# Splitting the tokens 256/288 and streaming the high and low inputs of 256 tokens in one 512-column matmul

## The chip, the cores and the metric

One core of one Trainium2 chip. The metric is device time in microseconds of one launch. Times of the kernel before: 2362.09, 2362.61 and 2363.95 us, median 2362.61 us.

## The reference, cut to what matters

Two layers of a streaming encoder act on 512 prompt tokens and 32 sample tokens, with a model width of 1024:

```python
for l in range(DEPTH):                       # DEPTH = 2
    mods = silu(c) @ ada_w[l] + ada_b[l]     # 9*1024 columns: shift, scale, gate of three sub-layers
    h = modulated_pre(x, ..., 0); x = gated_post(x, swiglu(h, w1, w3, w2), ..., 0, 0.5)
    h = modulated_pre(x, ..., 1)
    z = h @ w_in[l]                          # queries, latent, retention q, k, v, gate
    # latent attention and retention on z, then
    x = gated_post(x, concat(o_mla, o_ret) @ w_out[l], ..., 1, 1.0)
    h = modulated_pre(x, ..., 2); x = gated_post(x, swiglu(h, w1, w3, w2), ..., 2, 0.5)
# modulated_pre: rms_norm(x)*g*(1+scale)+shift;  swiglu: (silu(h@w1) * (h@w3)) @ w2, D_FF = 2816
```

Everything is float32. The kernel gets near float32 precision from matmuls of type fp32r by splitting each factor in a high part (rounded to fp32r) and a low part (the rest), and adds three products: high weight with high input, high weight with low input, low weight with high input.

## The kernel before, in words

Activations lie feature-major: 128 features on the partitions, T = 544 tokens along the free axis. A weight tile is 128x128 and turns one block of 128 input features into 128 output features. For each such tile and input block the kernel runs one **k-step** (`tile3`, L662): the 544 tokens are cut in two halves of HT = 272, one per PSUM bank, and each half gets three matmuls, six in all. Where the result needs a shift term, the second half carries 4 more columns (HB = 276), in which the product of weights and shift appears. An output tile is an accumulation over 8 k-steps (up projections, z, output projection) or 22 (down projection), into two neighbouring banks.

Stages of a layer: up projections of the first FFN (`up`, L765, two output tiles w1 and w3 for each of 22 features), its down projection (`out_tiles`, L787, 8 tiles, the last by `last_tile`, L813, one half after the other), a turn-over (norm, gate, new h; `first_tiles`, L714, starts the next stage while h is being made), the mixer's 21 z tiles (`z_tile`, L855), attention and retention, the mixer's output projection, and the second FFN in the same way.

Around PE each engine has its own program in a fixed order:

- **SP** loads weight chunks in `raw`, two slots, and in the down stages the tiles of `ada_w` (a ring of four) between them.
- **ACT** makes `w_hi` of each chunk (`high` L1172, `high_at` L1178, both wait for the chunk of that slot to be used up), and after that, in the same program, evacuates: `tile` in `up` (L1294: silu, cast to `u_hi`), `z_out` (L1350), `tile` in `out_tiles` (L1317: square, scaled copies to `o_buf`). An evacuation that waits holds the next `high`.
- **POOL** makes `w_lo` of each chunk after that (`low`, L543) and adds squares.
- **DVE** multiplies the PSUM results with the inverse root-mean-square `rinv` (`ffn` L1640; `z_scaled` L1689) and copies the four bias columns next to them, does the gating, the rotary embedding (`turn`, L1725, whose operations stand between the calls of `z_scaled`), in the down stages the modulation products (`ada_group`, L1551), and the residual updates (`turn_over`, L1580).
- **PE** waits for `lo_done` of a chunk before its tile, for bank evacuation (`up_out`, `z_mul`, `out_ev`), and in the last tile's second half, at k = 2, for `ada_done` of all modulation products of the stage (`half_sums`, L690). `z_tile(3)` waits for the evacuation of z tile 1 (L870).

In the mixer ACT's order is: `high` of chunk z + 2, then `z_out` of tile z, which waits for DVE's `z_mul`. So the weights of tile z + 3 come only after DVE has multiplied tile z. In the early tiles a `square` follows each `z_out` (L1368).

```python
for t in range(2):                                    # tile3, L667
    n = slice(t * HT, t * HT + width[t])
    pe.matmul(ps[:, bank + t, 0:width[t]], wh, hi[:, n], start=start, stop=False)
    pe.matmul(ps[:, bank + t, 0:width[t]], wh, lo[:, n], start=False, stop=False)
```

## Time and profile before

| | |
|---|---|
| timed runs | 2362.09, 2362.61, 2363.95 us (median 2362.61) |
| profiled execution | span 2360.0 us from its first to its last instruction; its own time outside the span is not listed, the median lies 2.6 us above the span |
| PE | busy 2304.0 us, 98% of the span |
| PE weight loads | 2184.5 us, 93% |
| DVE | 1220.4 us, 52% |
| POOL | 880.6 us, 37% |
| ACT | 821.1 us, 35% |
| DMA queue q1 | 262.44 MB, 33.1% of 16 engines |
| mean granted TensorE clock | 0.981 |

Busy matmuls overlap, since each is shown from its start until its result has passed the array, so 98% says that PE rarely waits, not that it streams all the time. How fast PE goes is read from the distance between the starts of its matmuls. Shares of DVE and ACT are averages over stages: in some stretches they are fully busy.

### The profile page before, as it was taken

How to read it: one execution, taken by the hardware profiler on the slowest of the kernel's cores; microseconds unless marked ns; L12 is line 12 of the kernel's file. 1: busy time of each engine (PE TensorE's matmuls, PEld its weight loads, DVE VectorE, ACT ScalarE, POOL GpSimd, SP SyncE). 2: the span in 40 equal slices, each digit the busy share in tenths (PEclk: the TensorE clock that was granted, in tenths of full speed). 3: DMA queues.
4: the chain of work that ended last, by engine and by line, in shares of the span. 5: the costliest groups of instructions: out<-in, count | busy, mean ns of one | idle time of the engine just before them, and what ended most of it. 6: DMA issues, size and time to landing. Idle time of an engine off the chain costs nothing.

```text
span 2360.0 us, 43873 instructions
## 1 busy us (share of the span) xinstructions
PE 2304.0 (98%) x17694; PEld 2184.5 (93%) x17694; DVE 1220.4 (52%) x2065; ACT 821.1 (35%) x1392; POOL 880.6 (37%) x382
## 2 busy tenths in 40 slices
PE   8999999999999999999999999999999999999998
PEld 7999999899558899999999999999984699999998
DVE  5333379877561533338153333996846624333502
ACT  4323332433454433332243333225343553332321
POOL 2344334343113344344434334443321143433352
PEclk7999999999999999999999999999999999999999
DMA  6222268322211122236312223882231022222422
GB/s 233 90 83 86 89 238 312 136 86 81 73 37 54 60 84 89 89 113 246 123 58 86 89 89 110 296 289 75 82 111 51 1 72 73 88 89 89 163 86 75
DMA packets 70948, 263.82 MB, mean 112 GB/s; under 512 B 8704, under 2 KB 10112, under 8 KB 70336
## 3 DMA queue, kind: packets, MB, share of 16 engines
q1 hardware_dynamic: 70848, 262.44, 33.1%
q8 instruction: 69, 1.13, 0.2%
q14 instruction: 31, 0.25, 0.0%
HBM read 258.96 MB, written 3.45 MB: 111 GB/s over the span
## 4 chain that ended last, share of the span: by engine, by line
PE 75%; issue 10%; DVE 5%; POOL 4%; ACT 3%; DMA 1%; SPq 1%; POOLq 0%; DVEq 0%; ACTq 0%
PE ps L673 21%; PE ps L669 20%; PE ps L670 20%; POOL w_lo L546 4%; DVE wide_v L1561 2%; PE ps L679 1%; PE ps L745 1%; PE ps L1090 1%; PE ps L832 1%; PE ps L834 1%; PE ps L833 1%; PE ps L975 1%; DMA x<-in_x 1%; PE ps L1113 1%; PE ps L1057 1%
## 5 line engine op out<-in xcount | busy, mean ns | idle before, releaser
L546 POOL TENSOR_TENSOR w_lo<-raw,w_hi 128x1024 fp32r<-128x1024 f32 (+1 forms) x304 | 785.9, 2585 | 1296.2 <-ACT w_hi L1183 947.4
L669 PE MATMUL ps<-h_hi,w_hi 128*128 128x272 f32 x3296 | 886.8, 289 | 3.7 <-POOL w_lo L546 3.7
L670 PE MATMUL ps<-h_lo,w_hi 128*128 128x272 f32 x3296 | 889.4, 287 | 0.0
L673 PE MATMUL ps<-h_hi,w_lo 128*128 128x272 f32 x3296 | 685.7, 289 | 0.0
L669 PEld LDWEIGHTS ps<-h_hi,w_hi 128*128 128x128 f32 x3296 | 619.1, 188 | 5.2 <-POOL w_lo L546 5.0
L670 PEld LDWEIGHTS ps<-h_lo,w_hi 128*128 128x128 f32 x3296 | 620.9, 188 | 0.2
L1183 ACT CAST w_hi<-raw 128x1024 fp32r<-128x1024 f32 (+1 forms) x236 | 269.3, 1141 | 830.6 <-PE ps L673 809.0
L673 PEld LDWEIGHTS ps<-h_hi,w_lo 128*128 128x128 f32 x3296 | 519.2, 188 | 0.0
L669 PE MATMUL ps<-u_hi,w_hi 128*128 128x272 f32 x1232 | 332.7, 288 | 1.0 <-POOL w_lo L546 1.0
L670 PE MATMUL ps<-u_lo,w_hi 128*128 128x272 f32 x1232 | 332.4, 289 | 0.0
L1561 DVE CUSTOM_DVE_ANT_0 wide_v<-ada_w,ps,ada_b 128x1024 bf16<-128x1024 f32 x256 | 309.0, 1285 | 22.7 <-DMA ada_w<-in_ada 18.2
L1652 DVE TENSOR_TENSOR wide_v<-ps,rinv 128x544 f32<-128x544 f32 x88 | 63.8, 725 | 437.3 <-PE ps L673 437.3
L673 PE MATMUL ps<-u_hi,w_lo 128*128 128x272 f32 x1232 | 255.2, 288 | 0.0
L1657 DVE SCALAR_TENSOR_TENSOR wide_v<-wide_v,wide_s 128x512 f32<-128x512 f32 (+1 forms) x176 | 193.7, 1139 | 105.2 <-ACT wide_s L1300 105.2
L669 PEld LDWEIGHTS ps<-u_hi,w_hi 128*128 128x128 f32 x1232 | 231.7, 188 | 1.9 <-POOL w_lo L546 1.9
L670 PEld LDWEIGHTS ps<-u_lo,w_hi 128*128 128x128 f32 x1232 | 232.1, 188 | 0.0
L673 PEld LDWEIGHTS ps<-u_hi,w_lo 128*128 128x128 f32 x1232 | 192.8, 188 | 0.0
L1303 ACT CAST u_hi<-wide_v 128x544 f32 (+1 forms) x88 | 57.1, 649 | 213.6 <-DVE wide_v L1657 213.6
L1587 DVE RECIPROCAL tok_inv<-tok_root 128x3 f32<-128x3 f32 x12 | 2.1, 176 | 247.4 <-ACT tok_root L1191 247.4
L1176 ACT CAST w_hi<-raw 128x1024 fp32r<-128x1024 f32 x68 | 71.2, 1047 | 125.5 <-PE ps L673 82.5
L1662 DVE TENSOR_TENSOR u_lo<-wide_v,u_hi 128x544 f32 x88 | 63.8, 726 | 80.1 <-ACT u_hi L1303 80.1
L1300 ACT ACTIVATE wide_s<-wide_s 128x512 f32<-128x512 f32 (+1 forms) x176 | 82.2, 514 | 4.6 <-DVE wide_s L1649 4.6
(284 smaller groups left out, 2642.3 us busy)
## 6 DMA issues: line engine op xcount, KB each, us to landing
raw<-in_w_up SPq DMA_DIRECT2D x176, 512.0 KB, 3.5
ada_w<-in_ada SPq DMA_DIRECT2D x128, 512.0 KB, 5.2
raw<-in_w_dn SPq DMA_DIRECT2D x64, 704.0 KB, 4.8
raw<-in_w_mix SPq DMA_DIRECT2D x64, 512.0 KB, 3.6
ada_first<-in_ada SPq DMA_DIRECT2D x10, 512.0 KB, 7.8
decay<-in_decay SPq DMA_DIRECT2D x2, 2048.0 KB, 8.7
ada_first<-in_ada_first SPq DMA_DIRECT2D x6, 512.0 KB, 11.4
x<-in_x SPq DMA_DIRECT2D x4, 544.0 KB, 17.2
```

What stands on the lines that cost most here:

```text
L546: pool.tensor_tensor(w_lo[:, slot, 0:width], raw[:, slot, 0:width], w_hi[:, slot, 0:width].bitcast(F32), ALU.subtract).then_inc(lo_done.se ...
L669: pe.matmul(ps[:, bank + t, 0:width[t]], wh, hi[:, n], start=start, stop=False)
L670: pe.matmul(ps[:, bank + t, 0:width[t]], wh, lo[:, n], start=False, stop=False)
L673: last = pe.matmul(ps[:, bank + t, 0:width[t]], wl, hi[:, n], start=False, stop=stop)
L1176: nc.scalar.copy(w_hi[:, slot, 0:width], raw[:, slot, 0:width]).then_inc(hi_done.sem, 1)
L1183: nc.scalar.copy(w_hi[:, k, 0:width], raw[:, k, 0:width]).then_inc(hi_done.sem, 1)
L1300: nc.scalar.activation(wide_s[:, f, at], wide_s[:, f, at], ACT.Silu, bias=wide_s[:, f, T + 2 * v:T + 2 * v + 1]).then_inc(up_silu.sem, 1)
L1303: nc.scalar.copy(u_hi[:, bass.ds(i * 2 + f, 1), :].rearrange("p a n -> p (a n)"), tmp_v[:, f, :]).then_inc(up_hi.sem, 1)
L1561: v_.tensor_tensor_reduce(junk[v], ada_w[:, t, :], c_psum(v), 1.0, ada_b[:, b0 + t:b0 + t + 1], ALU.mult, ALU.add, mods[:, v, n0 + t:n0 + ...
L1652: v_.tensor_tensor(halves(tmp_v[:, f, :]), pair(4 * f + 2), halves(rinv[:, :]), ALU.mult)
L1657: v_.scalar_tensor_tensor(out=wide_v[:, f, at], in0=wide_v[:, f, at], scalar=wide_v[:, f, T + 2 * v:T + 2 * v + 1], in1=wide_s[:, f, at], ...
L1662: v_.tensor_tensor(u_lo[:, at, :].rearrange("p a n -> p (a n)"), tmp_v[:, f, :], u_hi[:, at, :].rearrange("p a n -> p (a n)").bitcast(F32) ...
```

## The change

The halves become TA = 256 and TB = 288 tokens. High and low parts of each input now lie in one buffer (`h_both`, `u_both`, `qn_both`, `mla_both`, `ret_both`), so that one matmul can stream the high and then the low part of the first 256 tokens against the high weights: 512 columns, into the two halves of one bank. The low half of that bank collects high weight x high input (and low weight x high input), the upper half high weight x low input. The two bank halves have to be added before use. ACT copies the low half to SBUF (`apart_sb` lies in `squares`, `apart_out` in `root`), DVE adds it to the upper half in place, and after that the 544 tokens lie contiguous over two banks, so that evacuations that took two or three instructions take one. The same holds for `first_tiles`, which writes high products to the low half and low products to the upper. `uq` and the last output tile of each projection keep three matmuls per part (`half3`).

```diff
-HT = T // 2
+TA = 256
+TB = T - TA
...
-            [("h_hi", [P, KD, HP], F32R), ("h_lo", [P, KD, HP], F32R)],
+            [("h_both", [P, 2, KD, HP], F32R)],
...
+        def part(b, t, more=0):
+            return ps[:, b + 1, 0:TB + more] if t else ps[:, b, 512 - TA:512]
+        def tokens(b, width=T):
+            return ps[:, b:b + 2, :].rearrange("p b n -> p (b n)")[:, 512 - TA:512 - TA + width]
+        def apart(b):
+            return ps[:, b, 0:TA]
...
+            def half3(bank, t, wh, wl, both, start, stop, more=0):
+                out, n = part(bank, t, more), slice(OFF[t], OFF[t] + WID[t] + (more if t else 0))
+                pe.matmul(out, wh, both[:, 0, n], start=start, stop=False)
+                pe.matmul(out, wh, both[:, 1, n], start=False, stop=False)
+                return pe.matmul(out, wl, both[:, 0, n], start=False, stop=stop)
...
+            def tile3_apart(bank, slot, kk, both, start, stop, more=4):
+                wh = w_hi[:, slot, kk * P:(kk + 1) * P]
+                wl = w_lo[:, slot, kk * P:(kk + 1) * P]
+                pe.matmul(ps[:, bank, :].rearrange("p (v n) -> p v n", v=2), wh, both[:, :, 0:TA], start=start, stop=False)
+                pe.matmul(apart(bank), wl, both[:, 0, 0:TA], start=False, stop=stop)
+                return half3(bank, 1, wh, wl, both, start, stop, more)
...
                 def tile(i, f, last_width, ahead=True):          # ACT, up
-                    for k in range(2) if ahead else ():
-                        high_at(l, base, i * 2 + f + 1, k, last_width if f else KD * P)
+                    for k in range(2):
+                        if ahead:
+                            high_at(l, base, i * 2 + f + 1, k, last_width if f else KD * P)
+                        else:
+                            used(l, base + k)
+                        nc.scalar.copy(apart_sb[:, k, :], apart(4 * f + 2 * k)).then_inc(up_apart.sem, 1)
...
                     act.wait_ge(w_used.sem, w_used.at(l, chunk0 + (m + 1) * per_tile))     # ACT, out_tiles
+                    nc.scalar.copy(apart_out[:, mm, :], apart(2 * mm)).then_inc(out_apart.sem, 1)
                     act.wait_ge(sq_added.sem, sq_added.at(l, j * SQ + N_EARLY + m - 1))
-                    nc.scalar.activation(halves(tmp_s[:, mm, :]), pair(2 * mm), ACT.Square).then_inc(out_sq.sem, 1)
+                    act.wait_ge(out_added.sem, out_added.at(l, j * (KD - 1) + m + 1))
+                    nc.scalar.activation(tmp_s[:, mm, :], tokens(2 * mm), ACT.Square).then_inc(out_sq.sem, 1)
...
                 def z_out(z, buf, dst, func=ACT.Identity):       # ACT, mixer
+                    used(l, MIX_C0 + z)
+                    nc.scalar.copy(apart_sb[:, buf, :], apart(z_bank(z))).then_inc(z_apart.sem, 1)
                     act.wait_ge(z_mul.sem, z_mul.at(l, z + 1))
...
+            def add_out(l, j, m):                                # DVE
+                dve.wait_ge(out_apart.sem, out_apart.at(l, j * (KD - 1) + m + 1))
+                b = 2 * (m % 2)
+                v_.tensor_tensor(part(b, 0), part(b, 0), apart_out[:, m % 2, :], ALU.add).then_inc(out_added.sem, 1)
+            def add_apart(b, slot, added, l, count):
+                v_.tensor_tensor(part(b, 0), part(b, 0), apart_sb[:, slot, :], ALU.add).then_inc(added.sem, 1)
+                dve.wait_ge(added.sem, added.at(l, count))
...
-                        v_.tensor_tensor(halves(tmp_s[:, f, :]), pair(4 * f), halves(rinv[:, :]), ALU.mult)
-                        v_.tensor_copy(wide_s[:, f, T:TW], biases(4 * f)).then_inc(up_out.sem, 1)
+                        dve.wait_ge(up_apart.sem, up_apart.at(l, 2 * n + 1))
+                        add_apart(4 * f, 0, up_added, l, 2 * n + 1)
+                        v_.tensor_tensor(wide_s[:, f, :], tokens(4 * f, TW), rinv[:, :], ALU.mult).then_inc(up_out.sem, 1)
...
+                    for i in range(ADA_A // ADA_RING):           # DVE, first FFN's down stage
                         ada_group(l, i, 16 + i * ADA_RING, i * ADA_RING, first_ffn=True)
+                        if i == 1:
+                            dve.wait_ge(ada_done.sem, ada_done.at(l, 2 * KD))
+                            post_columns(l, 0)
+                        if i % 3 and i < 11:
+                            add_out(l, 0, 2 * (i // 3) + i % 3 - 1)
...
                 def z_scaled(z):
-                    dve.wait_ge(w_used.sem, w_used.at(l, MIX_C0 + z + 1))
+                    dve.wait_ge(z_apart.sem, z_apart.at(l, z + 1))
...
-                    v_.tensor_tensor(halves(z_tmp[:, z % 2, 0:T]), pair(bank), halves(rinv[:, :]), ALU.mult)
-                    v_.tensor_copy(z_tmp[:, z % 2, T:TW], biases(bank)).then_inc(z_mul.sem, 1)
+                    add_apart(bank, z % 2, z_added, l, z + 1)
+                    v_.tensor_tensor(z_tmp[:, z % 2, :], tokens(bank, TW), rinv[:, :], ALU.mult).then_inc(z_mul.sem, 1)
```

In the second FFN's down stage `add_out` of tiles 0, 1, 2, 3, 4, 5 and 6 stands behind modulation groups 0, 1, 2, 3, 4, 5 and 5 (in the last layer only groups 0 and 1 exist). In the mixer the seven `add_out` stand behind all other DVE work.

## Rows read from the trace of the kernel before

**Rows 1.** The page: busy time, and the chain that ended last.
```profile
PE 2304.0 (98%) x17694; PEld 2184.5 (93%) x17694; DVE 1220.4 (52%) x2065; ACT 821.1 (35%) x1392; POOL 880.6 (37%) x382
PE 75%; issue 10%; DVE 5%; POOL 4%; ACT 3%; DMA 1%; SPq 1%; POOLq 0%; DVEq 0%; ACTq 0%
```
**Rows 2.** Groups by line and shape: line, instruction, count, busy us, mean ns.
```profile
L669 PE MATMUL ps<-h_hi,w_hi 128*128 128x276 f32 x1648 | 477.7, 290 | 0.0
L669 PE MATMUL ps<-u_hi,w_hi 128*128 128x272 f32 x1232 | 332.7, 288 | 1.0 <-POOL w_lo L546 1.0
L669 PE MATMUL ps<-ret_hi,w_hi 128*128 128x272 f32 x112 | 30.4, 289 | 0.0
L669 PE MATMUL ps<-mla_hi,w_hi 128*128 128x272 f32 x112 | 30.2, 288 | 0.0
```
**Rows 3.** Timeline of ACT: start us, length us; weight casts that wait for PE.
```profile
401.70 1.38 ACT L1183 CAST w_hi<-raw 128x1408 fp32r<-128x1408 f32 x1 [5.48 <-PE ps L673]
...
426.56 1.38 ACT L1183 CAST w_hi<-raw 128x1408 fp32r<-128x1408 f32 x1 [6.91 <-PE ps L673]
...
813.76 1.05 ACT L1183 CAST w_hi<-raw 128x1024 fp32r<-128x1024 f32 x1 [4.99 <-PE ps L673]
...
825.84 1.05 ACT L1183 CAST w_hi<-raw 128x1024 fp32r<-128x1024 f32 x1 [4.90 <-PE ps L673]
```
**Rows 4.** Window at half clock (PEclk 0.50), PE's timeline in it, and float32 matmuls.
```profile
777.00:780.40 3.40, 1.95 (x8) 1.75 (x8) 2.65 (x8) 3.40 (x9) 2.37 (x1) 0.50 0.18 74
...
779.07 0.43 PE L728 MATMUL ps<-h_hi,w_hi 128*128 128x272 f32 x1
...
779.53 0.43 PE L728 MATMUL ps<-h_hi,w_hi 128*128 128x272 f32 x1
...
604.68 3.60 PE L920 MATMUL ps<-kv,k_tok 128*128 128x512 f32 x8
608.12 1.45 PE L930 MATMUL ps<-w_ukv,kv 128*128 128x512 f32 x3
```
**Rows 5.** Timeline of DVE and ACT in the z tiles of layer 0.
```profile
521.34 0.72 DVE L1695 TENSOR_TENSOR z_tmp<-ps,rinv 128x544 f32<-128x544 f32 x1 [0.50 <-PE ps L673]
...
572.93 0.72 DVE L1695 TENSOR_TENSOR z_tmp<-ps,rinv 128x544 f32<-128x544 f32 x1
...
574.60 1.04 ACT L1176 CAST w_hi<-raw 128x1024 fp32r<-128x1024 f32 x1
```
**Rows 6.** Windows: DVE's busy time in one stretch of the z tiles; PE after it.
```profile
545.00:557.00 12.00, 12.00 (x96) 11.79 (x94) 11.81 (x15) 3.88 (x6) 5.21 (x2) 1.00 0.28 83
...
578.15 0.39 PE L669 MATMUL ps<-h_hi,w_hi 128*128 128x272 f32 x1 [0.72 <-POOL w_lo L546]
```
**Rows 7.** Timeline of ACT and DVE at the first z tiles.
```profile
474.30 0.71 DVE L1695 TENSOR_TENSOR z_tmp<-ps,rinv 128x544 f32<-128x544 f32 x1
474.41 0.73 ACT L1352 ACTIVATE zq<-z_tmp 128x512 f32<-128x512 f32 x1 [3.23 <-DVE z_tmp L1696]
475.38 0.66 ACT L1357 ACTIVATE wide_s<-zq 128x544 f32<-128x544 f32 x1
476.25 0.72 DVE L1695 TENSOR_TENSOR z_tmp<-ps,rinv 128x544 f32<-128x544 f32 x1 [1.17 <-PE ps L673]
```
**Rows 8.** Timeline at the end of the first down stage: last DVE products, PE's half sums.
```profile
434.23 1.29 DVE L1561 CUSTOM_DVE_ANT_0 wide_v<-ada_w,ps,ada_b 128x1024 bf16<-128x1024 f32 x1
436.31 0.72 PE L686 MATMUL ps<-ones,squares 128*128 128x1 f32 x6
```
**Rows 9.** Timeline at the third down tile: ACT waits, PE's first matmul.
```profile
337.74 0.84 ACT L1330 ACTIVATE o_ffn<-ps,mul_post 128x272 f32<-128x272 f32 x2 [9.25 <-DVE mul_post L1575]
343.39 0.40 PE L669 MATMUL ps<-u_hi,w_hi 128*128 128x272 f32 x1 [0.27 <-POOL w_lo L546]
```
**Rows 10.** Groups by shape nearest to the added operations.
```profile
L1605 DVE TENSOR_TENSOR x<-x,ps 128x272 f32<-128x272 f32 x96 | 42.0, 438 | 3.3
L1330 ACT ACTIVATE o_ffn<-ps,mul_post 128x240 f32<-128x240 f32 x28 | 13.0, 463 | 0.0
```

More of the change, by code:

```diff
@@ L664, in tile3 @@
+            def tile3(bank, slot, kk, both, start, stop):
                 wh = w_hi[:, slot, kk * P:(kk + 1) * P]
                 wl = w_lo[:, slot, kk * P:(kk + 1) * P]
[L666 to L670 removed]
@@ L671, in tile3 @@
-                for t in range(2):
-                    n = slice(t * HT, t * HT + width[t])
-                    last = pe.matmul(ps[:, bank + t, 0:width[t]], wl, hi[:, n], start=False, stop=stop)
-                return last
+                half3(bank, 0, wh, wl, both, start, stop)
+                return half3(bank, 1, wh, wl, both, start, stop)
+            def tile3_apart(bank, slot, kk, both, start, stop, more=4):
[4 more added lines that the diff above has]
+                return half3(bank, 1, wh, wl, both, start, stop, more)
@@ L860, in z_tile @@
                     for k in range(KD):
[L861 removed]
+                        last = tile3_apart(bank, slot, k, h_both[:, :, k, :], k == 0, k == KD - 1)
                     last.then_inc(w_used.sem, 1)
@@ L1940, in _ @@
                 mixer(l)
+                for m in range(KD - 1):
+                    add_out(l, 1, m)
                 turn_over((l, 1, o_mix), (l, 2))
```

195 lines of the change are left out of this document (95 added, 100 removed).

## The prediction, made before the changed kernel was run

> **What bounds the kernel now.** The page's busy shares come first: PE 98%, DVE 52%, and 75% of the chain that ended last is PE [rows 1]. So the pace of PE's matmuls is the first term, and the question behind it is where another engine is already just in time. The groups by shape give the number of k-steps. L669 runs twice in each: 1648 x 2 calls with h make 1648 k-steps, u 616, the mixer's output projection 56 + 56, in all **2376** that become `tile3_apart` [rows 2]. Of the 1648, the loops give 1344 to the up projections (42 tiles x 8, four times) and 304 to the z tiles (19 x 8, twice).
>
> The pace: in the up stage two weight casts that wait for PE lie 12.08 us apart, 16 k-steps, so 755 ns each. In the down stage 24.86 us hold 33 k-steps, 753 ns each [rows 3]. At 2.4 GHz the columns alone would take 1644 / 2.4 = 685 ns and 1632 / 2.4 = 680 ns. So each of the six matmuls takes about 12 ns more than its columns. At the lower clock (0.50) two matmuls of 272 take 0.46 us, 230 ns each against 227 for the columns [rows 4]: there the excess is gone. The float32 matmuls, which stream at half rate, take 3.44 / 8 = 430 ns for 512 columns, against 427: also nearly nothing [rows 4]. The excess thus shows only where the stream (113 ns) is short and fast.
>
> **Term 1: five matmuls in place of six.** The columns stay the same (512 + 256 + 3 x 292 = 1644). What the sixth matmul and its weight load are worth isn't in the trace, so it is bounded:
>
> - nothing, if the excess goes with columns streamed at this rate and not with instructions;
> - 12 ns, if it is the same for each matmul;
> - 37 ns, if short matmuls are held to about 125.5 ns each whatever their width, while one of 512 streams at 213 + 3: 755 - (216 + 4 x 125.5) = 37.
>
> Between them the widths speak: the up step has 12 columns more than the down step, 5 ns of streaming, and takes only 2 ns more. That lies between a floor (0) and a fixed excess (5), so I take the middle between 12 and 37, **25 ns**. TensorE: Matmul & The Clock Gate in the Trainium skill (Back-to-back issue gap) gives N/2.4 + 2.5 ns per matmul; by it six would now take 700 ns where the rows show 755, and the saving would be 2.5 ns. The measured pace decides here, but the rule is a rival below.
>
> **Term 2: where a faster PE is not asked for.** Four places.
>
> *z tiles.* From 521.34 us on DVE never waits again until z tiles 16 and 17 at 572.93 [rows 5]; it is full of rotary operations, 11.81 of 12 us [rows 6]. The multiply of tile 16 frees ACT, which casts chunk 19 at 574.60, and PE resumes at 578.15 after a wait [rows 5, 6]. So the end of the z stage is DVE's, and each addition before it counts. One z tile now has an add of 256 columns in PSUM (0.44 us by L1605, [rows 10]; start to start about 0.4 once the wait for its own result is in) and loses the bias copy (0.07), so +0.4 us with the pipelining wait: 8 tiles from 9 to 16, 3.2 us. The start of the stretch moves too. DVE no longer starts on PE's signal but behind ACT's cast (1.05) and a copy (0.46, [rows 10]): +1.5. And at z tile 1 ACT copies the low half only after scaling and squaring tile 0: before, tile 1's multiply began at 474.30, in front of ACT's tile-0 work [rows 7]; now it is z_mul(0) at 474.8, scaling 0.95, square 0.66, copy 0.4, add and multiply 1.2: about 478.1. PE's z tile 3 waits for that and would have started when tile 2 was done, 476.2 [rows 7]: +2.0 us. Tiles 7 to 9, the latents' root in between, take the 2.0 and the 1.5 minus PE's gain by then (8 tiles x 8 x 25 ns = 1.6) and minus the 0.5 that DVE waited: about 2.1 in all with the adds at 7 and 8. So the z stage ends 3.2 + 2.1 = **5.3 us later** in each layer, and only the last two tiles' 16 k-steps of 152 gain.
>
> *First FFN's down stage.* The 48 modulation products keep DVE busy until 435.5, 0.8 us before PE's half sums, which wait for all of them [rows 8]. Seven `add_out` of 0.45 make 3.15 us, and the stage's first product starts 0.5 later, as ACT's copy precedes the last silu: DVE ends 125.7 + 3.65 = 129.4 us behind the stage's start (309.8) where PE was at 126.5. PE waits there however fast it was: **+3.0 us** in each layer, and its 308 k-steps gain nothing.
>
> *Second FFN's down stage.* ACT evacuates tile 0 only when `mul_post` is there (a 9.25 us wait until 337.74); cast, then POOL's low part, then PE's tile 2 after a wait at 343.39 [rows 9]. One or two adds (0.45 each) stand before it: tile 2 starts **0.85 us later**, the 44 k-steps before it gain nothing, 110 do. Twice.
>
> *Clock.* PE now stands still 3 to 5 us at the half sums. In the turn-over around 777 us the granted clock was at 0.50 after waits of that kind, for 3.4 to 6.8 us [rows 4]; 227 instead of 125.5 ns per matmul over 3.4 us loses 1.5 us, over 6.8 us 3.1. I take 2.5, twice.
>
> **Costed at nothing.** The adds and copies in the up stage: one feature's chain is cast 1.05, copy 0.46, add 0.44, multiply 0.7, gating 2.2, cast 0.65, in all 5.5 us before ACT is free, where a tile takes 5.8 us; and the next chunk has 2 us of slack behind that. If that cover goes, ACT's lateness reaches POOL's `w_lo` and PE. The output projection: copy, add, square, two copies are 3 us against a bank needed 6 us later. Merged instructions save DVE and ACT time off the path. The split 256/288 moves 0.4 us from one half of the last tile to the other; bounds -3 and +3 us over all six turn-overs. SP's queue issues the same DMAs in the same order; the `ada_w` loads behind later products can hold a `w_dn` load, with some 6 us in hand.
>
> **The sum.** K-steps that count: 1344 + 2 x 16 + 2 x 110 + 112 = 1708. Gain 1708 x 25 ns = 42.7. Costs 2 x 5.3 + 2 x 3.0 + 2 x 0.85 + 2 x 2.5 = 23.3. Net -19.4 us against the span of 2360.0, 2340.6; the median lies 2.6 above the span: **2343 us**.
>
> **Rivals.**
>
> - *Floor for short matmuls* (37 ns): 63.2 us gained. z costs 4.5 (more gain by tile 9), clock 3: 9 + 6 + 1.7 + 6 = 22.7. Net -40.5: 2322. For it: the flat step from 680 to 685 ns of columns, no excess at half clock. Against: a float32 weight load paces nothing at 427 ns, so no row shows the floor itself. Chance 0.20.
> - *Fixed 12 ns per matmul*: 20.8 gained; z costs 6.2, clock 2: 12.4 + 6 + 1.7 + 4 = 24.1. Net +3: 2366, no difference that counts. For it: it is the plain reading of 755 - 685. Against: the same excess is missing at half clock and in float32. Chance 0.22.
> - *Slower: DVE's chains without the gain.* The mechanism is DVE's queue in the z stage, its 48 products in the down stage: the price is 14.4 + 6 + 1.7 + 3 = 25 us if a k-step saves nothing (the excess goes with columns, as a stream slowed by the weight load beside it would show). It decides when a k-step saves less than 25 / 1708 = 14 ns. Then 2388. For it: DVE's full windows [rows 5, 6] and 0.8 us of slack [rows 8] are facts, the 25 ns a guess. Against: 12 columns more cost 2 ns, not 5. Chance 0.15. The Trainium skill's rule above, which leaves 2.5 ns for the sixth matmul, would gain 4 and land at 2383, beside this rival; its pace is contradicted by the 755 ns.
> - *The change doesn't do what it says*: the 512-column matmul, whose moving operand is two pieces far apart, costs more than its columns. At 25 ns more per step it ends like the last. Chance 0.05; no row has such an operand on the fp32r path.
>
> **How the numbers follow.** Forecast 0.38, with its own range 2333 to 2355. A measurement of this kernel can tell about 0.2%, 4.7 us, from no change. Faster: the forecast, the floor and a tenth of the fixed case, 0.60. Same: 0.14. Slower: 0.26, the last two rivals and a third of the fixed case. The range from 2316 to 2378 holds forecast, floor and fixed case with the unknown waits, and leaves out most of the two slower cases.
>
> **What would show it.** Casts that wait for PE in the up stage 16 x 730 = 11.7 us apart (11.5: floor; 11.9: fixed; 12.1: nothing). Starts of a 512-column matmul and the next 216 ns apart, or 225. PE's wait before z tile 19 longer, its first z tiles with a new gap of 2 us behind tile 2. In the first down stage a new wait of PE at L695 of 3 to 5 us and clock 0.50 behind it. Wrong would be: no wait there, DVE waiting for PE in the z tiles beyond tile 9, or new waits for `w_lo` in the up loops.

## The result, and the profile after

The changed kernel takes **2387.86 us** (median of 4 runs, 2387.33 to 2388.86) against 2363.28 for the kernel before beside it: ratio 1.0102, 95% interval 1.009 to 1.0114. It is **slower by 1.0%**. The forecast was 2343 us, faster. The profiled execution has a span of 2387.1 us against 2360.0. So the two traces differ by 27 us, where the medians differ by 24.6; the profiled execution of the changed kernel was its slowest.

The page, where [rows 1] stand for before:

```profile
PE 2307.4 (97%) x15288; PEld 2078.8 (87%) x15288; DVE 1249.4 (52%) x2108; ACT 888.5 (37%) x1610; POOL 882.7 (37%) x382
PE 75%; issue 11%; DVE 6%; POOL 4%; ACT 3%; DMA 1%; SPq 1%; POOLq 0%; DVEq 0%; ACTq 0%
```

2406 matmuls and weight loads fewer, and PE is busy 3 us *longer*. The groups by shape of the changed kernel, for [rows 2]; columns as there:

```profile
L698 PE MATMUL ps<-h_both,w_hi 128*128 128x512 f32 x1648 | 653.9, 397 | 11.5 <-POOL w_lo L564 7.8
L684 PE MATMUL ps<-h_both,w_hi 128*128 128x292 f32 x1648 | 491.4, 298 | 0.0
L699 PE MATMUL ps<-h_both,w_lo 128*128 128x256 f32 x1648 | 460.0, 279 | 0.0
L1586 DVE TENSOR_TENSOR ps<-ps,squares 128x256 f32<-128x256 f32 x218 | 94.2, 432 | 600.3 <-ACT squares L1321 530.2
```

The change does what it says: 1648 matmuls of 512 columns on `h_both` (the others read `u_both`, `mla_both` and `ret_both`), 218 additions of 0.43 us in the up stages and z tiles. The mean lengths overlap (a matmul is counted until it has drained), so the pace is read from starts. PE's timeline in an up loop of the changed kernel (start us, length us):

```profile
299.67 0.39 PE L698 MATMUL ps<-h_both,w_hi 128*128 128x512 f32 x1
299.90 0.28 PE L699 MATMUL ps<-h_both,w_lo 128*128 128x256 f32 x1
300.02 0.30 PE L683 MATMUL ps<-h_both,w_hi 128*128 128x292 f32 x1
300.15 0.30 PE L684 MATMUL ps<-h_both,w_hi 128*128 128x292 f32 x1
300.29 0.30 PE L685 MATMUL ps<-h_both,w_lo 128*128 128x292 f32 x1
300.42 0.39 PE L698 MATMUL ps<-h_both,w_hi 128*128 128x512 f32 x1
```

From 299.67 to 300.42 is one k-step, 0.75 us. Over the loops from 100 to 300 us the mean gaps between starts are 234 ns for 512 columns, 117 for 256, 134.6 for 292. Two casts on ACT that wait for PE, 16 k-steps apart, say the same with more digits:

```profile
285.52 1.05 ACT L1204 CAST w_hi<-raw 128x1024 fp32r<-128x1024 f32 x1 [4.64 <-PE ps L685]
...
297.60 1.05 ACT L1204 CAST w_hi<-raw 128x1024 fp32r<-128x1024 f32 x1 [4.72 <-PE ps L685]
```

12.08 us, as in [rows 3]: 755 ns with five matmuls, 755 with six. **The sixth matmul and its weight load were worth nothing.**

Where the 27 us are, from the starts of PE's stages in the two traces (us):

| stage | before | after | more |
|---|---|---|---|
| up stages, four together | 1116.7 | 1117.8 | 1.1 |
| first FFN's down stage to the mixer's tile 0, layer 0 | 137.5 | 146.2 | 8.7 |
| the same, layer 1 | 137.4 | 145.5 | 8.1 |
| z tiles, layer 0 | 143.0 | 148.2 | 5.2 |
| z tiles, layer 1 | 142.7 | 147.6 | 4.9 |
| q and attention, both | 264.6 | 266.2 | 1.6 |
| output projections, both | 105.4 | 103.6 | -1.8 |
| second FFN's down stages and what follows them | 275.7 | 275.1 | -0.6 |

(The 1.6 us of the attention part are not the change's: that part takes 131.5 or 133.1 us in one layer or the other of several of the kernels below, without a pattern. The up stages' 1.1 lie in the later ones.)

Two stages make it, and PE's waits name them. The waits of the changed kernel (line waited at, cause, us in total, times, longest):

```profile
PE ps L698 <- POOL w_lo L564: 12.2, 10, 1.5
PE ps L711 <- DVE mods L1599: 10.5, 2, 5.2
PE ps L698 <- DVE z_tmp L1742: 3.6, 2, 1.8
```

The second and third didn't exist before. The second is PE's half sums at the end of each first down stage, waiting for DVE's modulation products. PE's timeline there, and windows around it (us, PE busy, PEld busy, DVE, ACT, POOL, granted clock, DMA share, GB/s), changed kernel:

```profile
441.50 0.98 PE L711 MATMUL ps<-ones,squares 128*128 128x1 f32 x4 [5.24 <-DVE mods L1599]
```
```profile
426.30:441.50 15.20, 9.05 (x75) 8.64 (x74) 15.16 (x29) 3.77 (x7) 4.59 (x2) 0.92 0.58 194
441.50:445.00 3.50, 3.50 (x15) 3.50 (x16) 0.60 (x7) 0.26 (x1) 0.00 (x0) 0.50 0.01 2
445.00:448.40 3.40, 3.40 (x16) 3.38 (x16) 1.44 (x4) 0.00 (x0) 0.00 (x0) 0.50 0.00 0
448.40:451.80 3.40, 3.40 (x24) 3.40 (x24) 3.26 (x10) 1.80 (x5) 0.67 (x1) 0.88 0.00 0
```

DVE is busy in 15.16 of 15.20 us while PE stands for 5.2; then PE runs at 0.50, the 1.2 GHz level, for 7.7 us: two whole windows, and the first 0.8 us of the third, whose mean is 0.88. In layer 1 the same wait of 5.2 us is followed by 6.2 us at 0.50. [Rows 8] had PE arrive 0.8 us *after* DVE. The third wait is z tile 3's for z tile 1's multiply; DVE and PE there:

```profile
484.80 0.43 DVE L1586 TENSOR_TENSOR ps<-ps,squares 128x256 f32<-128x256 f32 x1 [1.95 <-ACT squares L1376]
486.05 0.50 PE L698 MATMUL ps<-h_both,w_hi 128*128 128x512 f32 x1 [1.82 <-DVE z_tmp L1742]
```

DVE in turn waits 1.95 us for ACT's copy. In layer 0 the clock falls behind this wait too (the window behind the wait, and the one after it):

```profile
486.80:490.20 3.40, 3.40 (x14) 3.11 (x14) 1.16 (x2) 2.11 (x5) 1.53 (x1) 0.50 0.00 0
490.20:493.60 3.40, 3.40 (x25) 3.22 (x24) 0.00 (x0) 0.85 (x2) 0.86 (x1) 1.00 0.41 139
```

That is 14 matmuls in 3.4 us where the next window has 25, some 1.5 us lost. In layer 1 the wait is as long, 1.82 us, and no such window follows. The rest of the z stage's loss lies at its end: PE's waits for `w_lo` there add up to 3.9 us in each layer, against 1.9 and 1.8 before. For layer 0 this makes 1.8 + 1.5 + 2.0 = 5.3 us where 5.2 were measured; in layer 1 about 1 us of the 4.9 stays unassigned.

### The profile page after: what moved, and what is told of

Its sections match the earlier page's. It is cut to its first block, busy times and chain, and to the rows that moved or that the text cites. A ratio compares the mean times of both kernels' runs of the same rounds, so it can differ in the third digit from the quotient of the medians.

```text
span 2387.1 us, 39345 instructions
## 1 busy us (share of the span) xinstructions
PE 2307.4 (97%) x15288; PEld 2078.8 (87%) x15288; DVE 1249.4 (52%) x2108; ACT 888.5 (37%) x1610; POOL 882.7 (37%) x382
## 4 chain that ended last, share of the span: by engine, by line
PE 75%; issue 11%; DVE 6%; POOL 4%; ACT 3%; DMA 1%; SPq 1%; POOLq 0%; DVEq 0%; ACTq 0%
PE ps L698 19%; PE ps L684 12%; PE ps L683 12%; PE ps L685 12%; PE ps L699 9%; POOL w_lo L564 3%; DVE wide_v L1599 2%; PE ps L705 1%; PE ps L771 1%; PE ps L1111 1%; PE ps L996 1%; DVE ps L1640 1%; DMA x<-in_x 1%; PE ps L1009 1%; PE ps L1134 1%
## 5 line engine op out<-in xcount | busy, mean ns | idle before, releaser
L698 PE MATMUL ps<-h_both,w_hi 128*128 128x512 f32 x1648 | 653.9, 397 | 11.5 <-POOL w_lo L564 7.8
L684 PE MATMUL ps<-h_both,w_hi 128*128 128x292 f32 x1648 | 491.4, 298 | 0.0
L685 PE MATMUL ps<-h_both,w_lo 128*128 128x292 f32 x1648 | 489.8, 297 | 0.0
L683 PE MATMUL ps<-h_both,w_hi 128*128 128x292 f32 x1648 | 489.1, 297 | 0.0
L699 PE MATMUL ps<-h_both,w_lo 128*128 128x256 f32 x1648 | 460.0, 279 | 0.0
L683 PEld LDWEIGHTS ps<-h_both,w_hi 128*128 128x128 f32 x1648 | 309.2, 188 | 75.2
L698 PEld LDWEIGHTS ps<-h_both,w_hi 128*128 128x128 f32 x1648 | 309.8, 188 | 13.6 <-POOL w_lo L564 9.3
L699 PEld LDWEIGHTS ps<-h_both,w_lo 128*128 128x128 f32 x1648 | 310.5, 188 | 0.2
L685 PEld LDWEIGHTS ps<-h_both,w_lo 128*128 128x128 f32 x1648 | 310.2, 188 | 0.0
L684 PEld LDWEIGHTS ps<-h_both,w_hi 128*128 128x128 f32 x1648 | 310.1, 188 | 0.0
L698 PE MATMUL ps<-u_both,w_hi 128*128 128x512 f32 x616 | 244.3, 397 | 4.3 <-POOL w_lo L564 4.3
L683 PE MATMUL ps<-u_both,w_hi 128*128 128x288 f32 (+1 forms) x792 | 235.4, 297 | 3.6 <-POOL w_lo L564 3.6
L684 PE MATMUL ps<-u_both,w_hi 128*128 128x288 f32 (+1 forms) x792 | 235.6, 297 | 0.0
L685 PE MATMUL ps<-u_both,w_lo 128*128 128x288 f32 (+1 forms) x792 | 234.5, 296 | 0.0
L683 PEld LDWEIGHTS ps<-u_both,w_hi 128*128 128x128 f32 x792 | 150.7, 190 | 32.3 <-POOL w_lo L564 4.5
L684 PEld LDWEIGHTS ps<-u_both,w_hi 128*128 128x128 f32 x792 | 150.9, 191 | 0.0
```

Source lines behind the costliest of these rows:

```text
L683: pe.matmul(out, wh, both[:, 0, n], start=start, stop=False)
L684: pe.matmul(out, wh, both[:, 1, n], start=False, stop=False)
L685: return pe.matmul(out, wl, both[:, 0, n], start=False, stop=stop)
L698: pe.matmul(ps[:, bank, :].rearrange("p (v n) -> p v n", v=2), wh, both[:, :, 0:TA], start=start, stop=False)
L699: pe.matmul(apart(bank), wl, both[:, 0, 0:TA], start=False, stop=stop)
```

## Experiments

The theory after the result (A): a k-step's time goes with its columns, not its instructions, and the slowdown is the added copies and additions in two places, the z tiles and the first down stage. The rivals: a saving that is there and eaten by waits; a 512-column matmul slower for its operand in two pieces; other parts of the change (split, layout) that cost. Times are medians; each ratio is to the kernel before, run on the same chip, with its 95% interval.

| kernel | us | before beside it | ratio |
|---|---|---|---|
| changed kernel | 2387.86 | 2363.28 | 1.0102 (1.009 to 1.0114) |
| two256 | 2388.61 | 2362.43 | 1.0105 (1.0089 to 1.012) |
| undo_z | 2379.45 | 2362.43 | 1.0068 (1.0054 to 1.0082) |
| undo_down0 | 2367.89 | 2362.43 | 1.0023 (1.0014 to 1.0032) |
| split_only | 2360.40 | 2362.43 | 0.9988 (0.9979 to 0.9997) |
| undo_z_down0 | 2359.58 | 2361.18 | 0.9990 (0.9981 to 0.9999) |
| z1_early | 2381.00 | 2361.18 | 1.0080 (1.0067 to 1.0094) |
| copy_first | 2382.87 | 2361.18 | 1.0090 (1.0076 to 1.0104) |
| two_moves | 2377.11 | 2362.55 | 1.0064 (1.0052 to 1.0076) |
| two_columns | 2359.11 | 2362.55 | 0.9985 (0.9976 to 0.9994) |
| bias_high | 2358.38 | 2362.55 | 0.9981 (0.9972 to 0.999) |

### two256: the sixth matmul back, and nothing else

```diff
-pe.matmul(ps[:, bank, :].rearrange("p (v n) -> p v n", v=2), wh, both[:, :, 0:TA], start=start, stop=False)
+pe.matmul(apart(bank), wh, both[:, 0, 0:TA], start=start, stop=False)
+pe.matmul(part(bank, 0), wh, both[:, 1, 0:TA], start=False, stop=False)
```

> The changed kernel with the 512-column matmul of each k-step split back into two of 256 columns with the same weights (high inputs into the half apart, low inputs into the token half); six matmuls and a sixth weight load as before the change, everything else (banks, copies, additions, 256/288) as in the changed kernel. Theory A, a stream of this type costs 0.46 ns per column whatever its width and an instruction costs nothing: 2388 us within 3, k-steps of 16 in the up stage 12.08 us as before. My forecast's step, 25 ns for the sixth matmul: 1708 k-steps that count make it 2388 + 43 = about 2430. A fixed 12 ns per matmul: about 2408. A rival, that the 512-column matmul with its operand in two pieces was slower than two of 256 (by 10 ns or more per k-step): below 2371.

Ratio 1.0105 against 1.0102: no difference, and 2376 matmuls and loads more. Its casts on ACT:

```profile
285.79 1.05 ACT L1205 CAST w_hi<-raw 128x1024 fp32r<-128x1024 f32 x1 [4.64 <-PE ps L685]
...
297.87 1.05 ACT L1205 CAST w_hi<-raw 128x1024 fp32r<-128x1024 f32 x1 [4.72 <-PE ps L685]
```

12.08 us again. This decides the first term by itself: 25 ns per k-step would be 43 us, even 12 ns would be 20. Nor is the operand in two pieces slow, since it takes what two matmuls take.

### undo_z: the z tiles back to six matmuls, no copy, no addition

```diff
 # PE, z_tile
-last = tile3_apart(bank, slot, k, h_both[:, :, k, :], k == 0, k == KD - 1)
+last = tile3(bank, slot, k, h_both[:, :, k, :], k == 0, k == KD - 1, 4)
 # ACT, z_out
-used(l, MIX_C0 + z)
-nc.scalar.copy(apart_sb[:, buf, :], apart(z_bank(z))).then_inc(z_apart.sem, 1)
 # DVE, z_scaled
-add_apart(bank, z % 2, z_added, l, z + 1)
 ...  (first_tiles of the mixer writes to the token halves; DVE waits for PE's tile, not for the copy)
```

> The changed kernel with the z tiles alone taken back to six matmuls into one token half each, without the copy on ACT and the addition on DVE; up, down and output stages stay changed. Theory A (DVE's and ACT's added work ends the z stage later, the sixth matmul is worth nothing): z stages 144.5 us instead of 149.4, so 2388 - 10 = 2378. Rival B (the z stage is longer for another reason, such as the wider second half or the new order of ACT's evacuations): 2388 within 2. Rival C (a k-step did save 10 to 25 ns, eaten elsewhere): z tiles slower by 152 x 2 x 10 to 25 ns = 3 to 7.6 us, so 2381 to 2386.

Ratio 1.0068: 0.0034 or 8 us gone. By PE's stages the z tiles take 142.4 and 143.5 us instead of 148.2 and 147.6, 9.9 us together. That is before's time (143.0 and 142.7): rival B, another cause in the z stage, falls. So does rival C, a saving eaten elsewhere, which wanted z tiles 1.5 to 3.8 us slower per layer than before. PE's waits for `z_tmp` are gone, and those for `w_lo` at the stage's end are back to 1.9 us.

### undo_down0: the first down stage back

```diff
 # PE, out_tiles: j == 0 is the first FFN's
-last = tile3_apart(2 * mm, ...)
+last = (tile3 if j in (0,) else tile3_apart)(2 * mm, ...)
 # ACT: copy to apart_out, wait for out_added
+if j not in (0,):
 # DVE, add_out
+if j in (0,):
+    return
```

> The changed kernel with the first feed-forward's down stage alone (both layers) taken back: six matmuls into the token halves, no copy on ACT, no addition on DVE between the 48 modulation products. Theory A (the seven additions and the waits for ACT's copies push the products past PE's half sums, and the standstill then costs PE its clock): down stage and half sums back to 126.5 us and the turn-over to 9.4, 8 to 9 us per layer: 2388 - 17 = 2371, no wait of PE for the products at the half sums, granted clock above 0.9 behind them. Rival B (the loads of the modulation weights are what come late, pushed by the other layout): the wait stays, 2386 to 2389. Rival C (only the wait goes, the clock falls anyway): 2388 - 11 = 2377.

Ratio 1.0023: 0.0079 or 19 us gone, the largest part. Down stage and turn-over take 136.6 us in both layers (after 146.2 and 145.5). PE at its half sums, and the windows behind them:

```profile
436.01 0.50 PE L715 MATMUL ps<-ones,squares 128*128 128x1 f32 x4
```
```profile
426.30:436.00 9.70, 8.83 (x74) 8.63 (x73) 9.05 (x22) 3.23 (x6) 4.52 (x2) 1.00 0.46 162
436.00:439.40 3.40, 3.40 (x30) 3.40 (x29) 0.62 (x3) 0.44 (x2) 0.00 (x0) 1.00 0.03 5
```

No wait, and the granted clock stays 1.00 where it was 0.50: 30 matmuls in 3.4 us, not 15. So the standstill costs twice, once as itself and once as the clock behind it, and with the wait both go. Rivals B (late loads) and C (the clock falls anyway) are out. (One stretch of 3.4 us at 0.50 later in the turn-over, from 456.8 us, is no part of it: the kernel before has it too, from 459.3 us.)

### undo_z_down0 and split_only: the two together, and all of it

undo_z_down0 is the two edits above together. split_only goes on: no 512-column matmul, copy or addition in the up stages, second down stages and output projections either.

> Both undone, the z tiles and the first feed-forward's down stage; up stages, second down stage and output projection keep the 512-column matmul, 1904 of the 2376 k-steps. Theory A (the two parts are all of the slowdown, and add up: -9 and -20 alone): 2388 - 29 = 2359, as split_only's 2360.4. Rival B (the up and second down stages cost or gain something too): a difference of over 4 us from split_only. My forecast's 25 ns would by now have shown as 1904 x 25 ns = 48 us, 2313.

> The split 256/288 and the operands with high and low in one tensor, but no 512-column matmul anywhere: six matmuls per k-step into the token halves, no copy and no addition in any stage; merged evacuations stay. Theory A (a k-step's time goes with its columns; all of the slowdown is the added copies and additions): 2388 - 10 - 17 - 1 and the output projection's 2 back = 2359 to 2363, no difference from the kernel before. Rival B (the new split or layout itself costs some us): 2366 to 2375. My forecast's term, 25 ns per k-step: about 2400.

0.9990 and 0.9988: both parts account for the whole slowdown, and add up (0.0034 + 0.0079 = 0.0113; together 0.0112). The 1904 k-steps that keep the five matmuls in undo_z_down0 neither gain nor lose against split_only. The split 256/288 with its merged evacuations is worth 0.1%, which the intervals just tell from nothing.

### z1_early: one copy moved on ACT

```diff
 # ACT, z_out
-used(l, MIX_C0 + z)
-nc.scalar.copy(apart_sb[:, buf, :], apart(z_bank(z))).then_inc(z_apart.sem, 1)
+for y in ((0, 1), (), (2,))[z] if z < 3 else (z,):
+    used(l, MIX_C0 + y)
+    nc.scalar.copy(apart_sb[:, y % 2, :], apart(z_bank(y))).then_inc(z_apart.sem, 1)
```

> The changed kernel with one instruction on ACT moved: the copy of z tile 1's half apart comes right behind that of tile 0, ahead of tile 0's scaling and square; nothing is removed. Theory A (2.1 us of PE's gap behind z tile 2 is this copy in ACT's queue, and DVE, which has little idle time from tile 7 to the end of the stage, carries it to the end): the gap behind z tile 2 falls from 2.1 to about 0.1 us and the stage ends 1.5 to 2.1 us sooner in each layer, 2388 - 4 = 2384. Rival B (DVE's root and latents in between swallow it, as the later part of the stage is bound by the additions alone): the gap goes but the stage's end stays, 2387 to 2388. Rival C (the gap has another cause): gap and time stay.

Ratio 1.0080, so about 5 us gone (0.0022). ACT's two copies now stand together, and DVE adds tile 1 right behind tile 0's multiply, 2.3 us sooner than at 484.80:

```profile
478.89 0.64 ACT L1377 COPY squares<-ps 128x256 f32<-128x256 f32 x2
...
481.85 0.73 DVE L1743 TENSOR_TENSOR z_tmp<-ps,rinv 128x548 f32<-128x548 f32 x1
482.49 0.42 DVE L1587 TENSOR_TENSOR ps<-ps,squares 128x256 f32<-128x256 f32 x1
```

PE's gap is gone, and the z tiles take 144.7 and 145.4 us, 3.5 and 2.2 less. That the first layer gave back more than the gap of 1.8 us is the clock: the changed kernel had 3.4 us at 0.50 behind the gap, about 1.5 us lost, and here the window at that place is at full clock:

```profile
486.80:490.20 3.40, 3.40 (x24) 3.19 (x23) 1.16 (x2) 1.09 (x3) 2.37 (x1) 1.00 0.03 6
```

So a single copy in the wrong place was over half of the z stage's loss (5.7 of 10.1 us). What is left goes with the additions and the other copies: PE's waits for `w_lo` at the stage's end are still 3.9 us here, and 1.9 in undo_z, which has neither additions nor copies. Which of the two holds them was not tested apart; that it is the additions on a full DVE is argued from [rows 5, 6].

### copy_first: the copy ahead of a cast in the down stages

```diff
 # ACT, out_tiles
-for k in range(2):
-    high_at(l, chunk0, m + 1, k, chunk_tiles * P)
+high_at(l, chunk0, m + 1, 0, chunk_tiles * P)
 act.wait_ge(w_used.sem, ...)
 nc.scalar.copy(apart_out[:, mm, :], apart(2 * mm)).then_inc(out_apart.sem, 1)
+high_at(l, chunk0, m + 1, 1, chunk_tiles * P)
```

> The changed kernel with ACT's copy of the half apart in the two feed-forward down stages moved ahead of the second of the two weight casts of each tile (before: behind both). Theory A (two of the seven additions find DVE waiting, 1.93 and 3.03 us, for a copy that stands behind a cast of 1.38 us; the rest of that wait is PE's tile end): DVE gains 1 to 1.4 us at each of the two, PE's wait of 5.5 us at the half sums becomes 2.7 to 3.5, and 2388 - 2 x 2.4 = about 2383. Rival B (DVE waits for the end of PE's tile, the copy's place hardly matters): 2387 to 2388. Rival C (a cast 0.36 us later makes POOL's low part and PE's next tile late): above 2390.

In the changed kernel two of the seven additions find DVE waiting for the copy, which stands behind a cast (timeline of DVE and ACT in the changed kernel, then that of DVE in copy_first, then PE's wait there: us in both layers together, times, longest):

```profile
378.75 0.43 DVE L1582 TENSOR_TENSOR ps<-ps,root 128x256 f32<-128x256 f32 x1 [1.93 <-ACT root L1349]
...
410.08 1.38 ACT L1204 CAST w_hi<-raw 128x1408 fp32r<-128x1408 f32 x1 [6.87 <-PE ps L685]
411.36 0.36 ACT L1349 COPY root<-ps 128x256 f32<-128x256 f32 x1
411.75 0.43 DVE L1582 TENSOR_TENSOR ps<-ps,root 128x256 f32<-128x256 f32 x1 [3.03 <-ACT root L1349]
```
```profile
378.09 0.43 DVE L1583 TENSOR_TENSOR ps<-ps,root 128x256 f32<-128x256 f32 x1 [0.66 <-ACT root L1348]
...
411.09 0.43 DVE L1583 TENSOR_TENSOR ps<-ps,root 128x256 f32<-128x256 f32 x1 [3.40 <-ACT root L1348]
```
```profile
PE ps L711 <- DVE mods L1600: 7.4, 2, 3.7
```

PE's wait fell from 5.2 to 3.7 us, by 1.5, not by the 2 to 2.8 expected. The first addition's wait shrank, but the second grew from 3.03 to 3.40: what it waits for is the end of PE's tile 5, which no cast delays. Half of the theory holds: the cast was worth 1.3 us once, and the rest is that `add_out` of tile 5 stands in DVE's list before PE has tile 5. Still the two stages with their turn-overs are 3.2 and 2.5 us shorter, more than the wait's 1.5, as the granted clock behind the shorter standstill came back sooner:

```profile
440.80:444.20 3.40, 3.36 (x18) 3.40 (x19) 0.64 (x7) 0.26 (x1) 0.00 (x0) 0.64 0.01 2
444.20:447.60 3.40, 3.40 (x25) 3.38 (x24) 2.13 (x6) 0.22 (x1) 0.00 (x0) 0.86 0.00 0
```

By the ratio, 1.0090, the gain is 0.0012, and the two intervals overlap. Both moves together:

> The changed kernel with both moves on ACT, that of z1_early (alone -6.5 against the changed kernel, beside runs of the kernel before) and that of copy_first (alone -4.5). Theory A (both are waits for ACT's order, in different stages): they add up, 2377. Rival B (one gives back the other, as the clock or the loads shift): 2380 or more. Either way slower than the kernel before, since the additions themselves stay.

1.0064, so 0.0038 or 9 us gone: they add up (0.0022 + 0.0012), and it stays slower than before, as theory A has it.

### pace, pace2, pace3: PE by itself

Three kernels with nothing but matmuls, with 128 x 128 weights where not said, each section behind a warm-up of 24 matmuls of 512 columns. Each ran once, pace3 on another chip than the other two. Their core (pace) is

```python
for i in range(48):
    last = pe.matmul(ps[:, i % 4, 0:n], wr[:, i % 4, :], xr[:, 0, i % KD, 0:n], start=True, stop=True)
```

> Matmuls alone; the whole computation is left out. Sections of 48 or 64 matmuls with 128 x 128 weights, each behind a warm-up of 24 of 512 columns, no other engine at work: fp32r with 512, 384, 272, 256, 128 and 64 columns, with two pieces of 256 far apart, with 32-column weights, and bf16 with 512 and 256. Theory A (column law, 0.46 ns per column at full clock and nothing per instruction): start to start 235 ns for 512, 177 for 384, 125 for 272, 118 for 256, 59 for 128 as long as the weight load does not take over; pieces as contiguous. Rival B (the excess over columns / 2.4 is contention with the other engines' work in the kernel): alone 512 columns take 213 to 216 ns and 256 take 107 to 110. Rival C (the weight load beside the stream slows it): 32-column weights give 0.42 ns per column where 128-column ones give 0.46. bf16: 0.42 ns per column if the slower pace belongs to fp32r, 0.46 if to every stream on this chip.

> Matmuls alone again; the whole computation is left out. Single widths 264, 276, 288, 292, 272 accumulating, and whole k-steps (16 each, banks and weights alternating as in the kernels) in the order of the kernel before (272 + 272, six matmuls), of the changed kernel (512 + 256 + 3 x 288, 290 or 292, five), with the 512 split into two of 256, and of split_only (3 x 256 + 3 x n, six). What is open: in the kernels 1644 columns take 755.0 ns per k-step in four different forms, 1632 take 750.0 or 753.3, and 1638 (two_columns) take 756.7, so 0.46 ns per column doesn't hold to a few columns. Theory A (the pace is PE's own): the same figures appear alone, 753 for old_272, 750 for new_288 and two_288, 755 for new_292 and split_292, 756.7 for new_290. Rival B (the other engines' traffic adds to it): all are shorter alone, by 10 to 15 ns (six times 123.3 = 740 for old_272; 230 + 117 + 3 x 131 = 740 for new_288), and five matmuls may be shorter than six by the 4 ns that one of 512 took less than two of 256.

> Matmuls alone a third time; the whole computation is left out. Alone, single widths in multiples of 16 took 117.0 (256), 123.3 (272) and 130.2 ns (288), 10 above columns / 2.4, but whole k-steps took 749.3 to 752.6 in every form, 8 to 12 ns above the sum of their widths. Which part of the mixture adds that: one bank for successive matmuls (one_bank, bank_5), the same weights again (one_weight, weight_5), the same input (one_input), another start of the input (input_272, input_264) or of the output (out_240), or different widths in a row (mixed_6, mixed_alt, mixed_5)? Theory A (it is the change of width or of start): mixed_6 at 749 per six and mixed_5 at 749 per five, one_bank and one_weight at 123.3. Rival B (successive matmuls into one bank): one_bank about 125.4, mixed_5 at 738, bank_5 at 749. Rival C (the weights): one_weight shorter or longer by 2 ns. If mixed_5 alone is 738 and mixed_6 742, the sixth matmul is worth 4 ns by itself and the k-step's form takes it back.

Mean start to start at full clock, ns, fp32r unless said:

| columns | ns | above columns / 2.4 |
|---|---|---|
| 256 | 117.0 | 10.3 |
| 264 | 121.6 | 11.6 |
| 272 | 123.3 | 10.0 |
| 276 | 126.6 | 11.6 |
| 288 | 130.2 | 10.2 |
| 292 | 135.0 | 13.3 |
| 384 | 174.9 | 14.9 |
| 512 | 230.0 | 16.7 |
| 512 in two pieces | 230.0 | 16.7 |
| 128 | 110.8 | 57.5 |
| 64 | 111.6 | 84.9 |
| 512, 32-column weights | 226.7 | 13.4 |
| 256, 32-column weights | 116.6 | 9.9 |
| bf16, 256 and 512 | 109.4, 215.8 | 2.7, 2.5 |

The pace is slower than the columns with no other engine at work, so rival B, contention, falls. The excess *grows* with the width: 10 at 256, 17 at 512. Hence one matmul of 512 saves not a fixed 10 ns against two of 256 but 4 (234.0 against 230.0). The same 256 columns took 118.3 in pace3, so such figures hold to about 1 ns. With 32-column weights the excess shrinks by 3.3 ns of 17 at 512 columns and 0.4 at 256, so rival C, the weight load, is not the main cause either. Below 256 columns there is a floor: 128 and 64 columns both take about 111 ns.

With bf16 the excess is 2.5 to 2.7 ns. That is the rule of the Trainium skill which the prediction set against the trace (TensorE: Matmul & The Clock Gate, Back-to-back issue gap), and it holds for bf16 here, not for fp32r. That section of the Trainium skill gives it as the gap of an isolated matmul, and about 131 ns at 512 columns for a stream of weight loads and matmuls. The bf16 part of pace is such a stream, and took 215.8.

In the 64-column section the granted clock fell to 0.50 while PE never stood still (windows of pace; it has no DVE, so the columns are us, PE, PEld, ACT, POOL, clock, DMA share, GB/s):

```profile
98.10:104.10 6.00, 6.00 (x56) 6.00 (x54) 0.00 (x0) 0.00 (x0) 1.00 0.00 0
104.10:107.50 3.40, 3.40 (x14) 3.15 (x14) 0.00 (x0) 0.00 (x0) 0.50 0.02 5
```

At that level, seen once, 64 columns took 213.5 ns and the 512 columns behind them 427: the floor doubles, and the excess over the columns is gone, as [rows 4] had shown for 272.

Whole k-steps in pace2, with banks, weights and order as in the kernels; its timeline for the form of the changed kernel with 288:

```profile
109.85 0.40 PE L203 MATMUL ps<-xr,wr 128*128 128x512 f32 x1
110.08 0.28 PE L205 MATMUL ps<-xr,wr 128*128 128x256 f32 x1
110.20 0.56 PE L171 MATMUL ps<-xr,wr 128*128 128x288 f32 x3
110.60 0.39 PE L203 MATMUL ps<-xr,wr 128*128 128x512 f32 x1
```

| form | matmuls | columns | ns alone | in a kernel |
|---|---|---|---|---|
| 272 x 6 (before, down) | 6 | 1632 | 752.6 | 753.3 |
| 512, 256, 3 x 288 (changed, down) | 5 | 1632 | 749.7 | 750.0 |
| the same, 512 as two of 256 (two256, down) | 6 | 1632 | 749.6 | 750.0 |
| 3 x 256, 3 x 288 (split_only, down) | 6 | 1632 | 749.3 | 753.3 |
| 3 x 256, 3 x 292 (split_only, up) | 6 | 1644 | 762.8 | 755.0 |
| 512, 256, 3 x 292 (changed, up) | 5 | 1644 | 759.4 | 755.0 |
| 512, 256, 3 x 290 (two_columns, up) | 5 | 1638 | 757.2 | 756.7 |

So the pace is PE's own, within 8 ns, and where the kernels differ only in the split of the 512 columns, as the changed kernel and two256, five matmuls are not faster than six. Alone they are in one form: with 3 x 292 columns five take 759.4 and six 762.8. Both figures differ from the kernels' 755.0; pace2 reads its 290 and 292 columns from input column 254 and 252, not 256, which may be why. The 753.3 of split_only's down stages, 749.3 alone, stays open as well.

Two of 256 and one of 512 differ by 4 ns, and 512, 256, 3 x 288 shows nothing of it. pace3 (272 columns, 123.3 as the base) narrows that: one bank for all 123.4, one set of weights 123.3, another output start 123.4, and accumulation (in pace2) 123.4, all nothing; but the same input each time 125.3, an input that starts at column 272 125.5, at 264 123.8. Of what was varied only the moving input changes the pace by more than the 1 ns of noise, by up to 2.2 ns per matmul, and a k-step reads the same inputs in close sequence. With the inputs rotating, mixed_5 (512, 256, 3 x 288) takes 743.9 and mixed_6 747.9: there the sixth matmul is worth its 4 ns. With the banks or the weights in the k-step's order (bank_5, weight_5) it stays at 743. All are still 6 ns above the sum of their single widths, 737.6 for five and 741.6 for six. Why the input costs what it does stays open, and so does the 6 ns.

### two_columns and bias_high: fewer columns instead of fewer instructions

If columns are the price, columns are what to take away. Both start from undo_z_down0; two_columns stores each shift column once instead of twice (290 columns where 292 were), bias_high leaves the 4 shift columns out of two of the three matmuls.

```diff
 # two_columns
-TW = T + 4
+TW = T + 2
-h_hi[:, :, T + 2 * v:T + 2 * v + 2]
+h_hi[:, :, T + v:T + v + 1]
 # bias_high, half3
 pe.matmul(out, wh, both[:, 0, n], start=start, stop=False)
+out, n = part(bank, t), slice(OFF[t], OFF[t] + WID[t])
```

> undo_z_down0 with the shift columns behind the tokens stored once instead of twice: 2 in place of 4, so each matmul of the second half in the up stages and z tiles has 290 columns, not 292. Same result. Theory A (0.46 ns per column): 3 x 2 x 0.46 = 2.8 ns per k-step, 1344 in the up stages count in full and the z tiles' 304 in part: 3.7 to 4.5 us less than undo_z_down0's 2359.6, so 2355 to 2356, faster than both kernels. Rival B (a matmul's time doesn't follow a few columns): 2359 to 2360.

> undo_z_down0 with the 4 shift columns left out of two of the three matmuls of the second half in the up stages and z tiles: the low parts of the shift's product are left out of the computation there. 8 columns fewer per k-step. Theory A: only the tiles with three matmuls per half and the 512-column ones of the up stage count, 8 x 0.46 = 3.7 ns times 1344 to 1648 k-steps: 4.9 to 6.1 us less than 2359.6, so about 2354. Rival B (a few columns don't matter): 2359 to 2360. If two_columns falls by 4.2 and this by 5.5, the law holds at both sizes.

Ratios 0.9985 and 0.9981 against undo_z_down0's 0.9990, within the intervals; neither lost 4 to 6 us. Their casts 16 k-steps apart, two_columns first:

```profile
285.91 1.05 ACT L1208 CAST w_hi<-raw 128x1024 fp32r<-128x1024 f32 x1 [4.65 <-PE ps L689]
...
298.02 1.05 ACT L1208 CAST w_hi<-raw 128x1024 fp32r<-128x1024 f32 x1 [4.74 <-PE ps L689]
```
```profile
285.38 1.05 ACT L1209 CAST w_hi<-raw 128x1024 fp32r<-128x1024 f32 x1 [4.62 <-PE ps L690]
...
297.44 1.05 ACT L1209 CAST w_hi<-raw 128x1024 fp32r<-128x1024 f32 x1 [4.71 <-PE ps L690]
```

12.11 and 12.06 us: 6 columns fewer took 1.7 ns *more* per k-step, 8 fewer 1.7 less (3.7 expected). So my law of 0.46 ns per column was wrong as a law. It is a fair mean between 256 and 512 columns, and no more; the first table above shows why, with 264, 276 and 292 dearer for their columns than 256, 272 and 288. two_columns computes all that the reference asks for and is the fastest such version by its ratio, 0.15% under the kernel before; undo_z_down0 and split_only can't be told from it.

## Why the prediction was wrong

**Term 1 failed, and with it the forecast.** The step is "between 12 and 37, 25 ns": a k-step saved 0 ns in the up stages and 3.3 in the down stages (and two256, with six matmuls and the same 750.0, shows that the 3.3 are not the instruction's). The error was to read the 70 ns by which 755 exceeds 685 as six times 12 per matmul, and take the lower bound of 0 as the unlikely end. The evidence for it was thin: that 12 columns more cost 2 ns and not 5 in [rows 3] was taken for a sign of a floor; pace and pace2 show it as the unevenness of widths, which is as large as the quantity argued from. The missing excess at half clock in [rows 4] was the better sign, as it speaks against a cost per instruction of 12 ns at both levels.

Of the rivals for this term, the floor exists, but at 111 ns, under the 117 that 256 columns take, not at 125.5; and a fixed cost per matmul is contradicted by an excess of 10 ns at 256 and 17 at 512 columns.

**The rival that ended slower was right in its mechanism**: 0 ns its condition, "the excess goes with columns" its reason, the added work in DVE's queue its cost. Its chance, 0.15, was too small. That 2388 came so close is in part luck, as its terms were off in both directions: it had 14.4 us for the z tiles, 6 for the first down stages, 1.7 for the second ones and 3 for the clock, and 10.1, 11.0, -0.6 and 5.8 were measured.

- *z tiles*, +5.3 per layer: 5.2 and 4.9 by the stages, 8 us for both by undo_z's ratio. The mechanism was right: the gap behind z tile 2 (2.0 forecast, a wait of 1.82 seen), a longer wait for `w_lo` at the stage's end, and no new one in the up loops. The match of the number is luck. The 5.3 had PE's gain of 1.6 us taken off, which did not exist; the end costs 2.0 us, not over 3; and in layer 0 some 1.5 us are the clock behind the gap, which the forecast didn't have there.
- *First down stage*, +3.0 per layer: the stage took 5.5 more (126.5 to 132.0 us up to the half sums). The mechanism was right, the term too small: DVE's seven additions were priced at 0.45 each and their waits at nothing, while two of them waited 1.93 and 3.03 us (3.40 in layer 1). Not all of that was new delay, as DVE had waited 1.5 us for a load of `ada_w` there before. A wait of DVE on PE's tile end in the middle of a queue that has 0.8 us in hand [rows 8] belongs in the sum.
- *Clock*, 2.5 twice: the turn-over grew by 3.2 and 2.6. Right in kind, with 0.50 for 7.7 and 6.2 us.
- *Second FFN's down stage*, +0.85 twice: both together took 0.6 less. Tile 2 does start 0.6 us later there (34.2 us behind the stage's start, 33.6 before), but the rest of the stage gained its 3.3 ns per k-step. ([Rows 9] are of the first FFN's stage; the second one has the same wait of ACT, 9.26 us.)
- *Costed at nothing*: the up stages' copies and additions cost nothing (undo_z_down0 keeps them and is at 0.9990). The output projection gained 0.9 per layer. The split is worth about -2 us for all, inside its bounds of -3 and +3.
- *The sum*: 1708 x 12 ns is 20.5, not 20.8, which changes nothing.
- *The range*, 2316 to 2378, left out the case that came. With the terms as measured (10.1 z, 16.8 down stages with clock), the added work costs 27 us against a gain of nothing.

## To carry to other kernels

A count of instructions on a full PE says nothing until a row shows that an instruction costs time apart from its columns; where the trace has no such row, a saving of nothing belongs in the middle of the estimate, and one run of the kernel with nothing but the form of that instruction exchanged settles it (two256). A stand-alone loop is a weaker judge: here it missed the kernels' k-step by up to 8 ns, twice what it was asked to tell. Work moved to an engine that is half idle on average is paid for in the stages where that engine is full or has under 1 us in hand: look there for every wait that the new instruction makes, for the order of the queue it enters, and for PE's clock behind the standstill. When a part of a change saves nothing, undo it stage by stage: here two of five stages held all of the loss.
